# Expert weights of a routed mixer: sixteen full tiles, or twelve tiles packed in quarters of 32 rows

## The reference, cut to what matters

```python
scores = jax.nn.sigmoid((t @ router_w).astype(jnp.float32))
sel = (scores + router_b.astype(jnp.float32)).reshape(-1, N_EXPERT_GROUPS, EXPERTS_PER_GROUP)
group_score = lax.top_k(sel, TOP_K)[0].sum(-1)
g_best = jnp.argmax(group_score, axis=-1)
sel_in = jnp.take_along_axis(sel, g_best[:, None, None], axis=1)[:, 0]
_, local = lax.top_k(sel_in, TOP_K)
ids = g_best[:, None] * EXPERTS_PER_GROUP + local
...
hid = jax.nn.silu(jnp.einsum('nd,edf->nef', t, w_gate)) * jnp.einsum('nd,edf->nef', t, w_up)
y = jnp.einsum('nef,efd->nd', hid * gates[:, :, None], w_down)
```

## Time and profile before

| | |
|---|---|
| median of three runs | 1193.12 us (1190.84 to 1193.57) |
| profiled execution, its own time | 1192.98 us |
| span of its instructions | 1191.1 us |
| TensorE busy | 1040.0 us, 87% |
| VectorE, ScalarE, GpSimd busy | 359.0, 220.7, 157.4 us |
| mean traffic of the DMA engines | 222 GB/s |

### The profile page before, as it was taken

How to read it: one execution, slowest core, us unless ns; L and a number is a source line. 1 busy time by engine, 2 the same in 40 slices (tenths; PEclk the granted TensorE clock), 3 DMA queues, 4 the chain that set the end, 5 groups by cost and what they waited for, 6 DMA issues and landing times.

```text
span 1191.1 us, 12728 instructions
## 1 busy us (share of the span) xinstructions
PE 1040.0 (87%) x4874; PEld 556.9 (47%) x4874; DVE 359.0 (30%) x815; ACT 220.7 (19%) x452; POOL 157.4 (13%) x163
## 2 busy tenths in 40 slices
PE   2888999998899959999999369999999779999960
PEld 1544455575545535545444134444655435455430
DVE  0200420126635661111111151440346631111116
ACT  4210100036611101111111152001210111111111
POOL 4000220007700010000000310010000010000014
PEclk9889999997999959999999779999999879999995
DMA  9889249745120197999986492110210488999936
GB/s 339 324 295 380 98 170 341 289 174 160 28 106 18 67 349 269 358 359 362 350 339 280 160 335 79 36 53 0 85 47 36 189 323 290 339 376 367 341 126 243
DMA packets 87049, 264.38 MB, mean 222 GB/s; under 512 B 7905, under 2 KB 19073, under 8 KB 73425
## 3 DMA queue, kind: packets, MB, share of 16 engines
q1 hardware_dynamic: 61552, 216.76, 49.6%
q0 software_dynamic: 10256, 34.29, 7.9%
q10 hardware_dynamic: 15184, 12.56, 3.4%
HBM read 231.28 MB, written 31.52 MB: 221 GB/s over the span
## 4 chain that ended last, share of the span: by engine, by line
PE 81%; DMA 11%; DVE 4%; ACT 2%; issue 2%; POOL 0%; SPq 0%; DVEq 0%; ACTq 0%; POOLq 0%
PE bank L1572 21%; PE bank L1658 21%; PE bank L1584 12%; PE bank L1670 10%; DMA ring<-in_ada_w 4%; PE bank L1542 3%; PE bank L1528 3%; PE bank L1652 3%; DMA bz<-in_ada_w 2%; DMA h_rows<-h_tok 2%; DMA ring<-in_sg_w_in 1%; PE bank L1597 1%; PE bank L1799 1%; PE bank L1874 1%; DMA uv<-y_rows,small 1%
## 5 line engine op out<-in xcount | busy, mean ns | idle before, releaser
L1572 PE MATMUL bank<-ring,h_feat 128*128 128x512 f32 x640 | 281.2, 599 | 6.1 <-DMA ring<-in_sg_w_in 5.4
L1658 PE MATMUL bank<-ring,uv 128*128 128x512 f32 x560 | 251.9, 604 | 3.5 <-ACT uv L857 2.2
L1572 PEld LDWEIGHTS bank<-ring,h_feat 128*128 128x128 f32 x640 | 121.3, 192 | 155.0 <-issue 154.1
L1658 PEld LDWEIGHTS bank<-ring,uv 128*128 128x128 f32 x560 | 106.2, 194 | 126.1 <-issue 122.8
L1584 PE MATMUL bank<-ring,h_feat 128*128 128x512 f32 x320 | 143.2, 598 | 0.0
L1670 PE MATMUL bank<-ring,uv 128*128 128x512 f32 x280 | 126.5, 595 | 3.0 <-ACT uv L880 1.6
L1584 PEld LDWEIGHTS bank<-ring,h_feat 128*128 128x128 f32 x320 | 58.9, 190 | 64.2 <-issue 64.0
L1309 DVE TENSOR_TENSOR uv<-uv,bank 128x256 f32<-128x256 f32 x32 | 13.5, 422 | 213.2 <-ACT uv L872 213.2
L1670 PEld LDWEIGHTS bank<-ring,uv 128*128 128x128 f32 x280 | 50.8, 191 | 55.1 <-issue 51.1
L744 POOL DMA_INDIRECT uv<-h_rows,small x35 | 33.0, 944 | 311.4 <-PE bank L1652 290.9
L1528 PE MATMUL bank<-small,h_tok 128*128 128x128 f32 x224 | 35.3, 307 | 30.4 <-ACT h_tok L1022 20.4
(11 more groups left out here) (199 smaller groups left out, 893.6 us busy)
## 6 DMA issues: line engine op xcount, KB each, us to landing
ring<-in_moe_w_gate SPq DMA_DIRECT2D x35, 1024.0 KB, 9.9
ring<-in_moe_w_up SPq DMA_DIRECT2D x35, 1024.0 KB, 12.9
ring<-in_moe_w_down SPq DMA_DIRECT2D x35, 1024.0 KB, 9.2
ring<-in_ada_w SPq DMA_DIRECT2D x16, 2048.0 KB, 14.3
y_rows<-uv SPq DMA_DIRECT2D x35, 512.0 KB, 8.9
ring<-in_na_w_in SPq DMA_DIRECT2D x4, 2048.0 KB, 18.2
bz<-in_ada_w SPq DMA_DIRECT2D x4, 2048.0 KB, 13.6
bz<-mod SPq DMA_DIRECT2D x16, 512.0 KB, 7.9
```

The source lines that it names most:

```text
L1572: last = mm(jbank(key)[:, :], HT[:, cc, P * t:P * (t + 1)], w[:, cc, :], start=cc == 0, stop=cc == DC - 1)
L1658: last = mm(bank[2][:, :], XT[:, b, cc, :], w[:, :, cc, :], start=cc == 0, stop=cc == DC - 1)
```

## The change

Experts are ranked by count and packed. Expert 0 keeps a full pass. The other 15 are sorted by their count, and the ranks 1 to 4 get four quarters (128 rows), ranks 5 to 10 three quarters (96 rows), ranks 11 to 15 two (64 rows). That is 48 quarters, 12 passes. `plan_tiles` cuts each pass into pieces of 1, 2 or 4 quarters that belong to one expert and are aligned to their own size. `gate_up` and `down` issue each matmul once for each piece, with 32, 64 or 128 stationary columns, and write the matching 32, 64 or 128 partitions of PSUM. The pieces of passes 0 to 11 are (in rows): 128 in passes 0 to 4; 64, 32, 32; then 64, 64; then 32, 32, 64; then 64, 32, 32; then 64, 64 in each of passes 9 to 11. With the counts above ranks 1 to 3 of layer 0 (162, 156, 146) still exceed 128 and nothing else exceeds its room, so there are three overflow tiles in layer 0 and none in layer 1, as before.

The load of expert 0 moves ahead of the wait for the output projection. The 15 others are loaded by rank, with the expert number read from `ids_i` by SyncE (`ranked_expert`), into five slots (two more in `h_feat`, `bz` and `h_tok`). The index table is made for 192 places, sorted by rank on VectorE, and permuted into passes by 21 matmuls on TensorE. `route_slots` moves behind the first pass. The loop over passes is written out. GpSimd's two last additions go to VectorE. `MAXOV`, the bound for overflow tiles, is 12 (was 9).

```diff
-NTILE = E + MAXOV
+QUARTERS = [4] + [4] * 4 + [3] * 6 + [2] * 5
+QUARTER_AT = [sum(QUARTERS[:i]) for i in range(E)]
+NPASS = sum(QUARTERS) // 4
+RANKED = E - 1
+OVERFLOW_AFTER = (11, 12, 15)
+MAXOV = 12
+NTILE = NPASS + MAXOV
+WSLOTS = 5
+PLACES = 192
-POOL_ADDS = (1, 3)
...
+def plan_tiles():
+
+    tiles = [[] for _ in range(NPASS)]
+    for p, n in enumerate(QUARTERS):
+        k = 0
+        while k < n:
+            at = QUARTER_AT[p] + k
+            size = max(w for w in (1, 2, 4) if at % w == 0 and k + w <= n and k // 4 == (k + w - 1) // 4)
+            tiles[at // 4].append((at % 4, size, p, k))
+            k += size
+    return tiles
...
+FIRST_PASS = [QUARTER_AT[p] // 4 for p in range(E)]
+LAST_PASS = [(QUARTER_AT[p] + QUARTERS[p] - 1) // 4 for p in range(E)]
...
+                load_gate_up(layer, 0, 0)
+                load_down(layer, 0, 0)
                 wait_job(sp, ("o", layer, TT - 1, 1))
...
-                load_expert(layer, 0, 0)
-                load_expert(layer, 1, 1)
-                sp.wait_ge(gathered[0], 16 * (6 * layer + 1))
-                load_expert(layer, 2, 2)
+                sp.wait_ge(ids_ready, 2 * layer + 1)
+                for p in range(1, WSLOTS):
+                    ex = ranked_expert(p)
+                    if p == 3:
+                        sp.wait_ge(logits_done, TT * (layer + 1))
+                        sp.wait_ge(h2_stored, 16 * TT * (layer + 1))
+                    if p == 4:
+                        sp.wait_ge(late_idx_mm, layer + 1)
+                    load_gate_up(layer, ex, p)
+                    load_down(layer, ex, p)
...
+                def refill(e):
+                    freed = [p for p in range(E - WSLOTS) if LAST_PASS[p] == e]
+                    ex = [ranked_expert(p + WSLOTS) for p in freed]
+                    sp.wait_ge(gu_mm, NPASS * layer + e + 1)
+                    for p, x in zip(freed, ex):
+                        load_gate_up(layer, x, p % WSLOTS)
+                    sp.wait_ge(down_mm, NPASS * layer + e + 1)
+                    for p, x in zip(freed, ex):
+                        load_down(layer, x, p % WSLOTS)
...
+                dve.wait_ge(pos_done, (TT + 1) * (layer + 1))
+                link(nc.vector.scalar_tensor_tensor(rank_key, cnt[:, 1:E], float(E), rank16[:, 1:E], ALU.mult, ALU.add))
+                tt(rank_oh, row(rank_key, RANKED), bc(rank_key, RANKED), ALU.is_gt)
+                red(rank_of, rank_oh, ALU.add)
+                dve.wait_ge(idx_mm, (TT + 1) * layer + TT)
+                nc.vector.tensor_copy(idx_i[:, 0:1], idx_low[:, 0:1]).then_inc(idx_ready, 1)
+
+                tt(rank_oh, bc(rank_of, RANKED), row(ranks, RANKED), ALU.is_equal)
+                oh_by_rank = rank_oh.rearrange("p e r -> p r e")
+                tt(by_rank, oh_by_rank, row(expert_no, RANKED), ALU.mult)
+                red(ids, by_rank, ALU.add)
+                nc.vector.tensor_copy(ids_i, ids).then_inc(ids_ready, 1)
...
+                dve.wait_ge(idx_mm, (TT + 1) * (layer + 1))
+                nc.vector.tensor_copy(idx_i[:, 1:NPASS], idx_pass[:, 1:NPASS]).then_inc(idx_ready, 1)
...
+                for e in range(1, NPASS):
+                    for q, n, p, k in TILES[e]:
+                        out = idx_pass[32 * q:32 * (q + n), e:e + 1]
+                        if k < 4:
+                            last = mm(out, ident[:, 32 * k:32 * (k + n)], tok_low[:, p - 1:p], start=True, stop=True)
...
-            def gate_up(b, s):
-                w = xslot(s)[:, 0:4096].rearrange("p (k c n) -> p k c n", k=2, c=DC)
+            def gate_up(b, tiles, slot):
                 for cc in range(DC):
-                    last = mm(bank[2][:, :], XT[:, b, cc, :], w[:, :, cc, :], start=cc == 0, stop=cc == DC - 1)
+                    for q, n, p, _ in tiles:
+                        w = gate_up_at(slot(p)).rearrange("p (k c n) -> p k c n", k=2, c=DC)
+                        last = mm(bank[2][32 * q:32 * (q + n), :], XT[:, b, cc, 32 * q:32 * (q + n)], w[:, :, cc, :],
+                                  start=cc == 0, stop=cc == DC - 1)
...
+                def weights_of(e):
+                    for p in sorted({p for _, _, p, _ in TILES[e]}):
+                        s = turn(p)
+                        pe.wait_ge(expert_in[s], 48 * (len(range(s, E, WSLOTS)) * layer + p // WSLOTS + 1))
```

More of the change, by code:

```diff
@@ L346, in build @@
         le, ovx = late(MAXOV * E).rearrange("p (o e) -> p o e", o=MAXOV), late(1 + MAXOV)
+        start, cap, excess, rank_key, rank_of, ids = late(E), late(E), late(E), late(RANKED), late(RANKED), late(RANKED)
+        rank_oh, by_rank = [late(RANKED * RANKED).rearrange("p (a b) -> p a b", a=RANKED) for _ in range(2)]
+        tok_low, tok_high = late(RANKED), late(RANKED)
         bank = [ctx.enter_context(nc.psum_tensor(f"bank{i}", [P, 512], F32)) for i in range(8)]
@@ L395, in expert_steps, with rounds @@
         def expert_steps(eng, body):
-            for e in range(4):
+            for e in range(NPASS):
                 body(e, e % 3, e // 3, (e - 1) // 3)
[L399 to L403, removed]
+        def rounds(s):
+            return len(range(s, NPASS, 3))
         v_normed, ring_free = sem("v_normed"), sem("ring_free")
-        expert_in = [sem(f"expert_in{s}") for s in range(3)]
+        expert_in = [sem(f"expert_in{s}") for s in range(WSLOTS)]
         gathered = [sem(f"gathered{s}") for s in range(3)]
@@ L600, in store_y @@
                         .then_inc(y_stored[s], 16)
[L603 to L613, removed]
+                def refill(e):
[7 more added lines that the diff above has]
+                        load_down(layer, x, p % WSLOTS)
+                for e in range(LAST_PASS[E - WSLOTS]):
+                    refill(e)
+                    store_y(e, e % 3)
                 sp.wait_ge(x_mid, 2 * TT * (layer + 1))
@@ L761, in _ @@
                             pool.wait_ge(ov[layer]["xt_mm"], o - 2)
-                        gather(E + o, s, ov[layer][f"gathered{s}"])
+                        gather(NPASS + o, s, ov[layer][f"gathered{s}"])
                 pool.wait_ge(slots_set, layer + 1)
@@ L1213, in out_and_route @@
                 dve.wait_ge(rc_in, 16 * (layer + 1))
+                for out in tile_oh:
+                    nc.vector.memset(out, 0.0)
                 link(nc.vector.memset(earlier, 0.0))
@@ L1292, in experts @@
             def experts(layer):
-                base = E * layer
+                base = NPASS * layer
                 def read_xt(b, n):
@@ L1700, in body @@
                         last.then_inc(late_idx_mm, 1)
-                    if not (isinstance(e, int) and e == E - 1):
+                    if e < NPASS - 1:
                         nxt = (b + 1) % 3
@@ L1705, in body @@
                         xt_transposes(nxt).then_inc(xt_mm, 1)
-                    if not (isinstance(e, int) and e == 0):
+                    if e > 0:
                         sums(e - 1, (b - 1) % 3)
@@ L1960, in shape_constants @@
     rc[:, 265:281] = np.arange(E, 0, -1)
-    rc[:, 281:297] = P * np.arange(E)
-    rc[:, 297:306] = np.arange(MAXOV)
-    rc[:, 306:434] = np.arange(P)
-    rc[:, 434:RC_N] = P * np.arange(NTILE)
+    at = 281
+    order = [np.arange(MAXOV), np.arange(PLACES), P * np.arange(NTILE), np.arange(RANKED), np.arange(1, E),
+             32 * np.array(QUARTER_AT[1:]), 32 * np.array(QUARTERS[1:])]
+    for row in order:
+        rc[:, at:at + len(row)] = row
+        at += len(row)
     rc[:, RC_N:] = np.eye(P)
```

235 lines of the change are left out of this document (135 added, 100 removed).

## The result

The changed kernel takes **1219.26 us** (median of 4 runs, 1214.27 to 1220.72) against 1192.34 us (median of 4 runs, 1190.84 to 1193.57): ratio 1.022, 95% interval 1.019 to 1.025, so it is slower. The profiled execution has a span of 1216.9 us where before had 1191.1, a difference of 25.8 us. The forecast said 1212, range 1152 to 1226.

What follows compares the result with a forecast made beforehand. TensorE was taken as the bound, transfers just behind. Two layers x (2.4 + 2.7 - 0.7 + 4.7 + 1.0) = 20.2, less 0.9, gives +19.3 on 1192.98: 1212 us, range 1152 to 1226.

Steps and rivals of the forecast that it cites:

- Mixed passes: Passes 5, 7 and 8: shapes of 64 and 32 run one behind the other, 2.00 us a step, 25.5 a pass.
- Rival 1: Passes 5, 7, 8: different shapes on disjoint partitions overlap, steps of 0.86 us, transfers bound, 1156 us; chance 0.22.
- rival 2: Passes of 64 and 64: pieces do not overlap with 512 moving columns, 10.3 us more each, 1294 us; chance 0.03.
- Sum of the passes: Expert stage: 12 passes cost 182.0 us against 182.7 for 16, so -0.7 us a layer.
- Index matmuls: Router: two index matmuls a token tile become four in two shapes, +2.4 us a layer (bounds 0.5 and 3.5).
- Router to pass 0: Before the first transposes: gather lands sooner, but the permutation matmuls come ahead, +2.7 us a layer (bounds +0.5, +5).
- Last weights: Ahead of pass 11: TensorE waits for rank 15's down, issued after pass 9's down, +4.7 us a layer.
- The clock behind it: Pass 11, after the idle wait: TensorE's clock may be low, 0 to 2.6 us, taken as +1.0 a layer.
- Tail: End of kernel: five tiles' additions on VectorE alone instead of partly on GpSimd, -0.9 us.
- Rival 3: Start and last weights cost next to nothing, mixed steps 1.90 us: 1194 us, no change; chance 0.05.

Runs made afterwards that it cites:

- one-shape: Changed kernel with passes 5, 7 and 8 using four pieces of 32 columns in gate, up and down: 1145.5 us, ratio 0.959.
- sorted kernel: Changed kernel with passes 5, 7 and 8 issuing all chunks of the 64-column piece first, then those of the 32-column pieces: 1204.44 us, ratio 1.008.
- reordered kernel: Changed kernel with SyncE issuing rank 15's gate and up right after pass 9's gate and up, its down right behind pass 9's down: 1217.57 us, ratio 1.019.
- one-shape kernel with the semaphore of its own: Changed kernel with 32-column pieces in passes 5, 7, 8, last weights issued earlier, and a separate semaphore for rank 15's down: 1122.46 us, ratio 0.939.

## Why the forecast held, and where it was off

**Mixed passes.** Right, in mechanism and size: 2.00 us a step forecast, 15.88 / 8 = 1.985 measured. Rival 1 (overlap) and rival 2 (64 and 64 do not overlap) are both refuted, by 15.88 and by 7.02; the one-shape and the sorted kernel show that the mixture alone costs it. The rows behind the 2.00 were of pieces that share partitions; that it holds for disjoint ones too was an inference, which only the result bears out. The Trainium skill (TensorEngine Tiling (Array Packing), Tiling Modes, Key Properties) says that a change of mode drains the engine; the trace agrees, and gives the price: 0.13 us a change between 64 and 32 columns, and no overlap across it even where the pieces write disjoint partitions.

**Sum of the passes.** -0.7 forecast, -2.8 and -2.7 measured at the wait ahead of the last gate and up. The forecast counted the last pass's four changes too, which stand behind that point (0.7), and took each mixed pass 0.15 us too dear; the transposes of hid ahead of pass 11 lie under the wait (0.4), and in layer 0 the first two bodies were 0.3 shorter. These make -2.5 of it.

**Index matmuls.** The term held for what it named: 0.93 and 1.14 us for 0.45, three times, is +1.9 against 2.4. What was missing is what a longer run of small matmuls does to the clock of the projection behind it: +1.7 us once in layer 0 and twice in layer 1. The forecast had no term for it, and the trace of before shows no such projection.

**Router to pass 0.** Forecast +2.7, measured +1.0 and +2.3. The permutation was sized too high: 4.11 us for its 42 records, not 5.2. The layers differ because the kernel before waited 9.73 us for the store of tokens in layer 0 and 8.46 in layer 1, and that wait is gone in both.

**Last weights.** The step that failed in size. The forecast named place and cause of the wait and took one landing for down alone, 4.7. It had not followed SyncE's queue: rank 15's gate and up stood in it 13.7 us behind their release. But the queue is not all of it: with the order mended the waits are still 8.5 and 6.0 us. The rest is that down is issued only when pass 9's down has run, and that one semaphore made gate and up wait for it; with a semaphore of its own the wait and the slow clock behind it are gone in both layers, 22 us.

**The clock behind it.** +1.0 forecast, inside its bounds of 0 to 2.6; measured 2.4 and 2.0, and 2.9 to 3.0 after the waits of the reordered kernel. It does not grow with the wait: 5.87 us idle were followed by 9.96, 9.65 us by 9.38.

**Tail.** -0.9 forecast; the additions gave 1.5, and 2.5 more came from the end behind the last addition. In the trace of before SyncE's stores wait 5.5 us for each of GpSimd's two additions, and tile 3's ends only at 1183.16, which would hold the last stores. The kernel before with that edit alone shows both gains.

**The total.** It came 6.5 us low in the profiled execution (25.8 against 19.3), and that is the net of larger errors. Too low over both layers were the last weights (by 8.3 us), the clock behind them (2.4) and the slow projections (5.1, forecast as nothing). Too high were the passes (4.1), the way from the router to pass 0 (2.1), the counted part of the index matmuls (1.1) and the tail (1.5). What is left is under 0.5 each. So the closeness of 1212 to 1219 is in part luck. The forecast's own range, 1198 to 1226, is narrower than its bounds added up, which run from 1194 to some 1231.

**Rival 1's price** would have been wrong as well: it took 367 GB/s for the ceiling of the transfers, and 1156 us for the faster case. With the mixture gone the engines moved 415 GB/s. Rival 3's words and its sum do not agree: it says that the last weights cost next to nothing, and its sum keeps 4.3 us a layer for them; without them it would be some 1185, not 1194.

## What to carry to other kernels

Pack a TensorE pass from pieces of one shape, even if that means cutting a wide piece into narrow ones and issuing more matmuls: with fp32 and 512 moving columns, four of 32 cost what one of 128 costs (7.00 and 6.87 us), one of 64 beside two of 32 costs more than double (15.88). Where the last operand of a stage can only be loaded late, give it a semaphore of its own, so that the work that does not need it covers it; and follow the issuing queue to the end of the stage, since what is free is not yet issued. A share of 1.00 of the DMA engines does not say how many GB/s are still to be had; take away the other bound and measure.

## What the runs showed of the hardware

- TensorE's clock can fall while TensorE is busy without a break. The window of the slow projection at 389.43 in the changed kernel:

```profile
389.00:399.00 10.00, 10.00 (x26) 4.77 (x25) 5.41 (x25) 0.22 (x1) 0.25 (x1) 0.83 0.13 52
```

  and the same window of before:

```profile
389.00:399.00 10.00, 10.00 (x28) 4.64 (x27) 5.93 (x25) 1.37 (x3) 0.11 (x1) 1.00 0.13 52
```

  Both are busy 10.00 of 10.00 us, at a granted clock of 0.83 and 1.00: in the first, for a part of it the clock is at the lower of its two levels, 1.2 GHz. Ahead of the slow projection stood the transposes, the logits and the index matmuls. With 0.4 to 0.9 us more of these than before, one to five of the six projections were slow, none when the index matmuls were moved away, and none in the kernel before. Which places are hit differs between traces of the same router, and nothing here shows why. The Trainium skill (TensorE: Matmul & The Clock Gate, Part 1) ties the higher clock to how busy the engine has been; here the profile's busy share stays full through the fall, so a row's busy share does not tell it.
- A change between 64 and 32 columns costs 0.13 us, the same in matmuls of gate and up and of down. A change from 64 or 32 to 128 columns shows as 0.20 (eight transposes 1.09 us instead of 0.89), one from 128 to 64 as 0.15 (7.02 instead of 6.87).
- The DMA engines show share 1.00 at 378 GB/s and 1.01 at 415, and 426 in the window 614 to 619. The Trainium skill (DMA: Bandwidth & Descriptors, Specifications) gives 435 GB/s as the fabric's ceiling; the windows of 5 us and more shown here stay under it, while single slices of 3 and 3.5 us read up to 444 (one-shape kernel with the semaphore of its own) and 439 (changed kernel).
